# Expert gates added into a table in DRAM by accumulating transfers instead of one-hot products, and the two halves of a gathered expert fetched as one row

## The reference, cut to what matters

```
s = einsum('bshpd,hpkd->bshpk', q, keys)          # 8 heads, 2 halves, 128 keys
top_s, top_i = top_k(s, 16)
cand_s = top_s[..., 0, :, None] + top_s[..., 1, None, :]
best_s, pos = top_k(cand_s, 16)                   # 16 experts a head, 128 a token
expert = cand_i[pos];  gate = softmax(best_s)
act = gelu(einsum('td,thkd->thk', h, u[expert]))
y   = einsum('thkd->td', gate * act * v[expert])
```

## Time and profile before

| | us |
|---|---|
| timed runs, median (lowest, highest) | 3629.14 (3623.7, 3633.84) |
| the profiled execution | 3645.58 |
| its span | 3643.8 |
| selection stage, about | 1515 to 2787 |
| combine stage, about | 2787 to 3643 |

### The profile page before, as it was taken

One profiled execution on the slowest core, in us unless ns is written; L12 is line 12 of the kernel. 1 busy time (PEld: TensorE's weight loads), 2 busy tenths in 40 slices (PEclk: granted clock), 3 DMA queues, 4 the chain that ended last, 5 costly groups with the idle time before them and its releaser, 6 DMA issues. The chain is left out here.

```text
span 3643.8 us, 47766 instructions
## 1 busy us (share of the span) xinstructions
PE 3276.6 (90%) x18306; PEld 2869.6 (79%) x18306; DVE 2473.2 (68%) x4437; ACT 1403.2 (39%) x2462; POOL 1355.1 (37%) x1028
## 2 busy tenths in 40 slices
PE   5899999799689899699999999999996988989988
PEld 2677776588568789699999999999995766767766
DVE  5134344368733378688888877888886877777777
ACT  3133344267521221145655645656551222222222
POOL 0000000000000000034566666555556888888884
PEclk8999999999889999899999999999998999999999
DMA  7411210111143301268999999999999999999997
GB/s 280 156 62 44 73 56 30 53 35 61 52 139 113 133 30 53 83 222 291 348 372 365 333 363 382 332 371 365 329 335 334 363 322 312 322 329 323 338 321 273
DMA packets 314883, 828.71 MB, mean 227 GB/s; under 512 B 35104, under 2 KB 115360, under 8 KB 309152
## 3 DMA queue, kind: packets, MB, share of 16 engines
q1 hardware_dynamic: 195872, 422.82, 32.7%
q0 software_dynamic: 118784, 402.85, 30.2%
HBM read 712.82 MB, written 112.72 MB: 227 GB/s over the span
## 5 line engine op out<-in xcount | busy, mean ns | idle before, releaser
L1636 POOL DMA_INDIRECT s_row<-in_u_rows,back_expert x256 | 357.2, 1395 | 1829.0 <-DVE back_expert L1809 1567.5
L84 PE MATMUL s_ps_a<-back_dense_hi,s_u_hi 128*128 128x384 f32 x2048 | 700.1, 342 | 40.0 <-DVE s_u_lo L1699 40.0
L86 PE MATMUL s_ps_a<-back_dense_hi,s_u_lo 128*128 128x384 f32 x2048 | 689.4, 337 | 0.0
L85 PE MATMUL s_ps_a<-back_dense_lo,s_u_hi 128*128 128x384 f32 x2048 | 688.8, 336 | 0.0
L84 PE MATMUL c_ps_y<-back_dense_hi 128*128 128x512 f32 x1024 | 415.9, 406 | 115.8 <-DVE back_dense_lo L2056 115.4
L2031 DVE SCALAR_TENSOR_TENSOR c_y<-c_row,c_w,c_y 128x1024 f32<-128x1024 f32 x256 | 328.9, 1285 | 190.2 <-DMA c_row<-in_v,back_expert 186.4
L1636 POOL DMA_INDIRECT s_row<-in_v,back_expert x256 | 339.1, 1325 | 252.1 <-DVE back_y L1833 196.1
L84 PEld LDWEIGHTS s_ps_a<-back_dense_hi,s_u_hi 128*128 128x128 f32 x2048 | 388.6, 190 | 40.9 <-issue 33.5
L85 PE MATMUL c_ps_y<-back_dense_lo,back_dense_hi 128*128 128x512 f32 x1024 | 409.0, 399 | 0.0
L86 PE MATMUL c_ps_y<-back_dense_hi,back_dense_lo 128*128 128x512 f32 x1024 | 408.9, 399 | 0.0
L85 PEld LDWEIGHTS s_ps_a<-back_dense_lo,s_u_hi 128*128 128x128 f32 x2048 | 388.4, 190 | 0.0
(11 more groups left out here) (331 smaller groups left out, 6492.9 us busy)
## 6 DMA issues: line engine op xcount, KB each, us to landing
s_u_raw<-in_u SPq DMA_DIRECT2D x128, 512.0 KB, 7.5
c_v_raw<-in_v SPq DMA_DIRECT2D x128, 512.0 KB, 6.5
act_scratch<-s_a SPq DMA_DIRECT2D x128, 384.0 KB, 9.1
gm_scratch<-s_gm SPq DMA_DIRECT2D x16, 2048.0 KB, 13.4
c_a<-act_scratch SPq DMA_DIRECT2D x128, 256.0 KB, 5.8
c_g<-gm_scratch SPq DMA_DIRECT2D x32, 1024.0 KB, 8.4
a_w<-in_w_ada SPq DMA_DIRECT2D x24, 1024.0 KB, 7.5
gate_scratch<-at_gate SPq DMA_DIRECT2D x32, 256.0 KB, 2.0
```

What stands on the lines that cost most here:

```text
L84: nc.tensor.matmul(out, w_hi, x_hi, start=first, stop=False)
L85: nc.tensor.matmul(out, w_hi, x_lo, start=False, stop=False)
L86: return nc.tensor.matmul(out, w_lo, x_hi, start=False, stop=last)
L1636: gp.indirect_dma_start(out=row[:, n % R], out_offset=None, in_=table, in_offset=bass.IndirectOffsetOnAxis(ap=keep.expert[:, g, k:k + 1], ...
```

## The change

Six things go together.

- **Gates.** The one-hot rows, their products, the transposes and the stores are gone. DVE computes for each of the 128 chosen experts of a token its place in the table `gm_scr`, now laid out chunk, expert, token (`slot`: expert times 512 plus the token's number). POOL then issues for each of tiles 0 to 3 128 accumulating indirect transfers of 128 elements of 4 bytes, one per token, which add the gates to the table. Scatter k of a tile waits until scatter k - 1 of the same tile has landed (`scattered`).
- **Clearing.** The table is filled with zeros in the attention stage: 16 transfers of 2 MB from a zeroed tile, one every four turns of that stage's SP queue.
- **Rows.** u and v of an expert lie side by side in one input (`uv_rows`); 256 fetches of 8 KB per partition replace 512 of 4 KB, into 8 buffers. A row is freed when its v half has been added.
- **Operands.** The token's row for the dot products is copied to PSUM by ACT, and the sum of a tile is accumulated in PSUM (`ps_rows`); ACT applies gelu to the dots of a chunk, multiplies by the gate, and copies the sums out.
- **Plan.** Tile 7 is chosen sixth instead of third; DVE's units are spread by a new rule up to chunk 125; `adds` says which scatters follow which fetch: none before fetch 15, one after each of 11 fetches, then two after 12, three after 43, and two after 174, always for the open tile with the fewest so far; a tile opens some fetches after it was chosen (fetches 15, 26, 38, 49).
- **Combine.** 6 raw buffers in place of 4, gates loaded per chunk in pieces of 2 KB, 10 row buffers in place of 8.

The core of the diff:

```
+    def gates_cleared(n):
+        if n == 0:
+            sp.wait_ge(zero_done, 1)
+        source = zero[:].rearrange("p (o t) -> p o t", o=1).broadcast_to([P, CLEARED, TB])
+        sp.dma_start(io["gm_scr"][n * CLEARED:(n + 1) * CLEARED].rearrange("c p t -> p c t"), source).then_inc(gm_zeroed, 16)
...
-            for n in range(2 * UNITS):
-                if n < UNITS:
-                    g, k, table = n // SEL, n % SEL, io["u_rows"]
-                else:
-                    g, k, table = n % GATHERED, (n - UNITS) // GATHERED, io["v_rows"]
...
+            def fetch(n):
+                g, k = n // SEL, n % SEL
+                if k == 0:
+                    gp.wait_ge(step, BEFORE[CHOICES.index(DENSE + g) + 1])
+                if n >= R:
+                    gp.wait_ge(used, n - R + 1)
+                gp.indirect_dma_start(out=row[:, n % R], out_offset=None, in_=io["uv_rows"],
+                                      in_offset=bass.IndirectOffsetOnAxis(ap=keep.expert[:, g, k:k + 1], axis=0)).then_inc(row_in[n % R], 16)
+
+            def scatter(tile, k):
+                if k == 0:
+                    gp.wait_ge(step, BEFORE[CHOICES.index(tile) + 1])
+                else:
+                    gp.wait_ge(scattered[tile], 16 * k)
+                gp.indirect_dma_start(out=gates, out_offset=bass.IndirectOffsetOnAxis(ap=slot[:, tile, k:k + 1], axis=0),
+                                      in_=dense_gate[:, tile, k:k + 1], in_offset=None, compute_op=ALU.add).then_inc(scattered[tile], 16)
+
+            for n in range(UNITS):
+                fetch(n)
+                for tile, k in adds[n]:
+                    scatter(tile, k)
...
+            for c in range(NK + 1):
+                here = rows[c] if c < NK else []
+                before = rows[c - 1] if c >= 1 else []
+                for n in here[:1]:
+                    dot(n)
                 if c + AHEAD < NK:
                     low(c + AHEAD)
+                for i in range(max(len(here) - 1, len(before))):
+                    for n in before[i:i + 1]:
+                        add(n)
+                    for n in here[i + 1:i + 2]:
+                        dot(n)
...
-                    if q in (1, 3):
-                        for g in groups[c][q // 2:q // 2 + 1]:
-                            gates(g)
```

More of the change, by code:

```diff
@@ L1509, in selection_plan @@
             ends[n] = c
[L1510 to L1517, removed]
+    last, taken = NK - 3, 0
+    other = [1.3 + 3.4 * len(parts[c]) for c in range(NK)]
+    whole = sum(other[:last + 1]) + 2.65 * UNITS
     for c in range(NK):
-        fit = int((sum(span[:c + 1]) * share - sum(other[:c + 1])) / 1.32)
-        upto = units if c == NK - 1 else min(units, max(fit, taken)) if c >= 5 else 0
+        fit = int((whole * (c + 1) / (last + 1) - sum(other[:c + 1])) / 2.65)
+        upto = UNITS if c >= last else min(UNITS, max(fit, taken)) if c > ends[0] else 0
+        if taken < SEL < upto:
+            upto = SEL
         rows[c] = list(range(taken, upto))
         taken = upto
-    return parts, turn, groups, rows, ends
+    upto = [sum(len(r) for r in rows[:c + 1]) for c in range(NK)]
+    opens = {upto[ends[CHOICES.index(tile)]] + 4: tile for tile in range(BOTH)}
+    adds, open_tiles, count, done = [[] for _ in range(UNITS)], [], [0] * BOTH, 0
+    for n in range(UNITS):
+        open_tiles += [tile for at, tile in opens.items() if at == n]
+        if not open_tiles:
+            continue
+        left = UNITS - 2 - n
+        due = (BOTH * SEL - done + left) // (left + 1) if left >= 0 else BOTH * SEL - done
+        for _ in range(min(due, len(open_tiles)) if left >= 0 else due):
+            tile = min((x for x in open_tiles if count[x] < SEL), key=lambda x: count[x], default=None)
+            if tile is not None:
+                adds[n].append((tile, count[tile]))
+                count[tile] += 1
+                done += 1
+    assert count == [SEL] * BOTH
+    return parts, rows, adds, ends
 def activate_and_select(nc, io, keep):
-    R = 6
+    R = 8
     AHEAD = 2
@@ L1534, in activate_and_select @@
     UNITS = GATHERED * SEL
-    parts, turn, groups, rows, ends = selection_plan()
-    chunk_of = {g: c for c in range(NK) for g in groups[c]}
-    blocks = BOTH * P // SPAN
-    PER_BLOCK = SPAN // GT
+    parts, rows, adds, ends = selection_plan()
+    upto = [sum(len(r) for r in rows[:c + 1]) for c in range(NK)]
     with ExitStack() as ctx:
@@ L1790, in part @@
                 elif j == 6:
-                    before = sum(c < n for c in DENSE_CHOICES)
-                    if before:
-                        dve.wait_ge(t_ready, before)
                     summed(0)
```

312 lines of the change are left out of this document (114 added, 198 removed).

## The result

| | before | after |
|---|---|---|
| timed runs, median (lowest, highest), us | 3627.03 (3623.7, 3633.84) | 3934.64 (3929.92, 3946.58) |
| the profiled execution, us | 3645.58 | 3934.63 |
| its span, us | 3643.8 | 3932.8 |

The ratio is 1.0832, with a 95% interval of 1.0804 to 1.086: 8.3% slower. The forecast was 3666 with a range up to 3800. The sign was right, the size was not, and the time lies outside the range; the nearest case was the much slower rival, 3828.

The account below looks back on a forecast made before the run. POOL was to replace PE as the selection stage's bound and keep bounding combine: combine's POOL start 39 us later, combine -4, attention +2, so +37 on 3645.6 gives 3683, or 3666 against the timed median; range 3560 to 3800.

Parts of the forecast that it names:

- the much slower rival: Selection stage: scatters cost POOL more than look-ups, or PSUM operands don't free it; at 1.59 each 3828 us; chance 0.17.
- step 3: Selection stage, units 56 to 255: 623 POOL instructions at 1.33 us, 829 us, landings mostly unwaited, last one at 2813.
- Steps 1 and 2: Selection stage on POOL up to unit 56: unit 26 at 1690 us, then unit 56 at 1984.
- wrong if scatters last longer than 1.1 us alone on POOL: Selection stage: sign set against the forecast, which priced a scatter as a four byte look-up, 0.94 us plus 0.30 gap.
- step 3's upper bound of 1.66: Selection stage: highest price of one POOL instruction, the stage's present 1.36 us plus 0.30 gap; 1.33 was taken.
- Step 2: Selection stage, units 26 to 56: 60 scatters wait for their tile's last to land, 4.9 us each, 294 us; unit 56 at 1984.
- 9 + 7, 14 + 2 + 5 and 22: Selection stage: waiting scatters of tile 1, tile 2 and tile 3, counted from the plan as 60.
- PE's part: Selection stage: 1024 one-hot products and 12 transposes go, 1078 us left; busy about 1085 with 200 idle behind u_lo.
- the bound of 100 us on DVE: Selection stage: PSUM operands cost DVE nothing, or at most 0.2 us x 512 = 100 us, bringing it to 1075.
- the -4: Combine stage: ten row buffers for eight remove POOL's 4.1 us of waits for free rows.
- The gap between the stages: Selection to combine: last row lands, then dot, gelu, weight, add, copy, 13 us, against 10.4 before.
- +2: Attention stage: 16 clearing transfers of 2 MB delay weight loads by 2 us, bounds 0 and 100.

Follow-up runs that it names:

- the counts 0, 256, 384 and 512: Changed kernel with 0, 256, 384 or all 512 of its scatters kept, each against the kernel before: ratios 0.948, 0.960, 1.021, 1.083.
- the spread: Changed kernel, its plan never giving one tile two scatters after the same fetch, 512 scatters kept; against the kernel before: 3878.88 us, ratio 1.064.
- the two-tile mixtures: Kernel before with one-row fetch, tiles 0 and 1 gated by scatters, 2 and 3 by one-hot products; buffers, sum, store order varied: ratios 0.999 to 1.0459.
- two-tile form with the sum in PSUM: Tiles 0 and 1 by scatters, 2 and 3 by one-hot products, seven row buffers, expert sum in PSUM; against the kernel before: 3660.11 us, ratio 1.0059.

## Why the prediction was wrong

**The failed step** is step 3, the price of one POOL instruction, and in it one sentence: "No row shows an accumulating transfer; as one of 128 elements I take it for a look-up." Steps 1 and 2 together landed where they were put. These are units 26 and 56 and the last fetch in POOL's timeline after (forecast 1690, 1984, 2813):

```profile
1692.30 0.98 POOL L1643 DMA_INDIRECT s_row<-in_uv_rows,back_expert  x1 [0.31 <-issue]
...
1983.26 1.00 POOL L1643 DMA_INDIRECT s_row<-in_uv_rows,back_expert  x1 [0.30 <-issue]
...
3063.45 1.00 POOL L1643 DMA_INDIRECT s_row<-in_uv_rows,back_expert  x1 [0.31 <-issue]
```

At unit 56 the forecast is off by 1 us; over the 623 instructions after it by 250. They took 3064.5 - 1983.3 = 1081 us, 1.735 each for 1.33. The kernel whose scatters only write shows what the premise gives. Busy time and gaps are (554.3 + 124.5 + 272.3 + 70.6) / 768 = 1.33 an instruction, and its same 623 instructions took 875 us, 31 of them waits for landings that step 3 had put at nothing. So of the 252 us by which step 3 was short, 206 go with the add and 46 would have been missed without it. The prediction's own sign, "wrong if scatters last longer than 1.1 us alone on POOL", is the one that came. The add itself costs 1.54 - 0.96 = 0.58 us of POOL per scatter in the timelines, 512 x 0.55 = 280 us by the groups (1.873 against 1.326 with the gaps), of which the time shows 1.0832 - 1.0173 = 0.066, some 240 us; some of the price hides the landings, whose waits fell from 181 to 137 us.

**The range** shared the fault. Its upper end, 3800, was set short of the much slower rival, 3828. That rival named the mechanism, but its price of 1.59 was today's contended price of a plain transfer, which bounds contention and not an operation that no row shows. Even step 3's upper bound of 1.66 gives only 623 x 0.33 = 206 more, 3872. With the measured prices the same sum gives 1984 + 200 x 1.37 + 423 x 1.87 = 3049. The Trainium skill (Collectives: The Full Stack, "The bandwidth ceiling") counts two read descriptors for an add where a copy has one. POOL's 1.54 for 0.96 goes that way, but it is 1.6 times as much. That it is this descriptor and not another cost of the add was not tried.

**Step 2** was right in sum and wrong in its parts, so its 1 us is luck. In the early stretch, by POOL's timeline after, a tile's next scatter is issued 3.2 to 3.3 us after its last:

```profile
1842.29 1.56 POOL L1651 DMA_INDIRECT gm_scratch<-s_dense_gate,s_slot  x1 [1.80 <-DMA gm_scratch<-s_dense_gate,s_slot]
1845.49 1.54 POOL L1651 DMA_INDIRECT gm_scratch<-s_dense_gate,s_slot  x1 [1.64 <-DMA gm_scratch<-s_dense_gate,s_slot]
1848.83 1.54 POOL L1651 DMA_INDIRECT gm_scratch<-s_dense_gate,s_slot  x1 [1.80 <-DMA gm_scratch<-s_dense_gate,s_slot]
```

That is less than the 4.9 taken. The DMA engines were busy for 0.63 there and not 0.90; whether that is why was not tried. What made the sum fit is what I had left out, the instructions between the waits: 30 fetches at 1.3 and the scatters that did not wait. (The list of scatters that wait, 9 + 7, 14 + 2 + 5 and 22, also adds up to 59 and not to 60.) Of the 137 us of waits 113.9 fell between 1690 and 2000, in 54 scatters, and none after; the prediction had put some 300. So step 3 was right to cost them at nothing for this kernel; where the scatters only write, 31 us of waits are left there.

**PE's part** was off as well, without cost. It was put at 1085 us busy and 200 idle behind u_lo and was 1202 busy, at a granted clock of 0.88 where the sum had today's 0.98, and 380 idle. With that much idle time it isn't the bound.

**What held.** That POOL, not PE, becomes the bound: shown by the counts 0, 256, 384 and 512, and by the spread, in which 64 us less of POOL's waits gave 70 us. That PSUM operands leave POOL alone: shown by the run with the token in SBUF, and the price of the dots there did not change (1218 for 1223; the add 1284, as before), so the bound of 100 us on DVE was not needed. The rule of the Trainium skill (SBUF — State Buffer, "Who interferes with whom") holds here by 2.23 against 1.57. The prediction's reading, that a transfer is stretched beside such an operation, needs one word more: only when it begins inside one. That PE alone would need 1078 us: 1066 in the run without scatters. The combine stage: 3080.32 to 3865.8 for its look-ups, as long as before to within 1 us, so that the -4 put on it was not seen. The gap between the stages was 16.9 us for 13. That clearing costs attention nothing: +2 was put, and the next stage's first load is issued at 688.4 us for 689.9 before.

**What stays open.** Why the one-row fetch alone is slower than the kernel before (1.026 and 1.029): the first of the two forms was short of rows, the second of gate blocks, and both store gates in pieces of half the size; a form with neither was not tried. So the 191 us that the run without scatters gains can't be split between the fetch and the one-hot products. Open too are what in an adding transfer takes POOL 0.58 us more, and whether the DMA engines or the waits for buffers hold the two-tile mixtures.

## What to carry to other kernels

An operation that no row of the trace shows has no price by likeness: before an engine that is to become the bound is given 512 of them, measure one, or take the range up to twice the nearest. Count what the new bound has to do in instructions and gaps, not in bytes, and compare with the room that it has: half of these scatters were nearly free, the other half cost 1.7 to 1.8 us each. When memory for one buffer is got by taking away another, look for the new wait before the old one's gain is counted: one gate block for two made ACT wait 280 us.

## What the runs showed of the hardware

- An indirect transfer of 128 elements occupies POOL for 0.93 to 1.00 us when it does not begin inside a DVE operation on two SBUF tensors, whether each is 4 bytes or 8 KB, read or written, and 1.54 us if it adds; 0.30 us lie between two.
- A transfer that begins inside a DVE operation on two SBUF tensors is longer by what is left of that operation, less some 0.1 us (2.23 for 1.55 with 0.79 left, 3.11 for 1.00 with 2.24 left). One that is under way when such an operation begins isn't stretched (1.54), and neither is one beside an operation with an operand in PSUM (1.57).
- Two accumulating transfers that wait for each other follow at 3.2 to 3.3 us in the stretch in which the DMA engines are busy for 0.63. In the two-tile form with the sum in PSUM, where the DMA engines are busy for 0.98 of the time, POOL waited 210 us for the landings of 256 of them.
- TensorE's granted clock was lower where PE stood waiting: 0.99 while PE was busy 1067 of 1085 us (no scatters), 0.88 over the stage after (1202 of 1560), 0.83 where PE was busy 205 of 300 us.
